# Who makes the low parts of the weight tiles: GpSimd or VectorE, in a streaming encoder block on one Trainium2 core

## The chip, the cores and the metric

The kernel runs on one core of one Trainium2 chip. The metric is device time in microseconds (us) from one launch; the times are medians of several executions. In the texts PE is TensorE, DVE is VectorE, ACT is ScalarE, POOL is GpSimd, and SP is SyncE, which here only issues transfers.

## The reference, cut to what matters

One layer of an encoder block for 512 tokens of width 1024, in float32. Three gated branches are merged, and then comes what this study is about: the output projection, a SwiGLU feed-forward part and a final norm.

```python
merged = gates[:, :, 0] * ya + gates[:, :, 1] * yb + gates[:, :, 2] * yc
x = x + merged @ w_out[l]                                   # 1024 x 1024
hf = _rms(x, g_ffn[l])
x = x + (jax.nn.silu(hf @ w_gate[l]) * (hf @ w_up[l])) @ w_down[l]   # 1024 x 2816, 2816 x 1024
return _rms(x, g_final)
```

## The kernel before, in words

**Splitting.** Each float32 matrix product is made from parts in fp32r. An operand is rounded (`hi`), and the rest `lo = x - hi` is kept as well; a product is then three matmuls, hi by hi, hi by lo and lo by hi (`product`, lines 1994 to 1996; `step`, lines 2416 to 2418, in the down projection). So each weight tile of 128 x 1024 passes four hands: SP loads it (`raw`), ACT rounds it (`w_hi`, `round_weights`, line 726; `round_unit`, line 1118), POOL or DVE subtracts (`w_lo`), and PE uses both. There are `NS = 2` slots for a tile and its parts. A load of tile t waits until the low part of tile t-2 is made (`next_weights`), and the rounding of tile t waits until PE has used tile t-2.

**Order of the tiles.** Tiles are numbered in one stream. `T_WO` to `T_WO + 7` are the eight tiles of the output projection, one for each of eight column groups `c`. `T_FF` to `T_FF + 15` are the tiles of the four "plain" pairs of the feed-forward part, four tiles a pair (gate 0, gate 1, up 0, up 1). After `T_ST` come `ST_TILES = 49` tiles for seven more pairs ("turns"), computed by a scheme with seven half-size products, and then eleven units `k` of the down projection, which share slots with the ring of the turns. A PE tile of the output projection or of a plain pair is 24 matmuls of 512 columns; a unit is 12.

**Who makes a low part.** A tile below `T_DVE = T_FF + 4` is made by POOL (`low_weights`, line 622, 128 x 1024 at once; before that `low_half`, line 627), and counted on `w_ready`. From `T_DVE` on it is DVE's: `low_plain` for the plain pairs, `low_weights(n)` for the turns, both through the helper `tt` (line 1217), counted on `w_ready_dve`. Of the units, 6 and 8 are DVE's and the other nine POOL's (line 716, in two halves with a semaphore each; unit 0 at once, line 713). `tile_low` and `low_done` turn a tile number into the count to wait for.

**DVE's program around it.** All engines run their instructions in the order written. DVE's, in order: (1) for c = 0 to 7: add the output projection's result to the residual (line 1653), make `hu_lo` (line 1657, waits for ACT's `hu_hi`), add up squares (`sqsum`, line 1217); (2) sixteen transposes of the residual (line 1664), some drains; (3) wait for `std` from ACT (line 735), RECIPROCAL to `rstd` (line 1670); (4) `scaled_gate(0, 0)` and `scaled_gate(0, 1)`, `scaled_up(0, 0)`, `low_plain(T_FF + 4)`, `scaled_up(0, 1)`, `low_plain(T_FF + 5)`, and the rest of the pairs; (5) in each turn some fifteen small combinations with `low_weights` among them; (6) `hidden_sums(10)` (four instructions of 128 x 256), `low_hidden(10)`, the low parts of units 6 and 8, then the low parts of the last stage (`low_three`).

**ACT's program around it**: for k = 0 to 7 round tile `T_WO + k + 2`, round `hu_hi`, square; round `T_FF + 2` and `T_FF + 3`; `std`; round `T_FF + 4`; SiLU; and so on. Before the units: round units 0 and 1, SiLU, units 2 and 3, `split_hidden(10)` (line 1023, waits for DVE's `hidden_sums(10)`), then the other units.

**POOL's program.** Beside the low parts POOL issues accumulating transfers between DRAM tensors (`weight_sums`, line 639), paced by waiting for each tile's low part, with three steps for each of 25 jobs. SP issues the plain copies that go ahead of them (`next_copy`, line 468), the loads of tiles (line 433 in the plain pairs) and, in the second plain pair, the eight stores of the transposed residual (`store_x1`, line 491: four behind the load of `T_FF + 4`, four behind the load of `T_FF + 5`).

**PE's program around it**: tiles `T_WO` and `T_WO + 1` interleaved, `T_WO + 2` to `T_WO + 7`, `T_FF`, a small product for the sum of squares, `T_FF + 1` to `T_FF + 15`, the turns, the units. Before each tile it waits for the tile's low part (`tile_ready`).

Of the kernel before, what the change touches and what calls it, by code (L numbers as in the profile page):

```python
# [21 lines left out]
WB = 512  # L22
# [7 lines left out]
TILE = 1024  # L30
# [16 lines left out]
T_WO = T_J2 + 14  # L47
# [4 lines left out]
T_ST = T_FF + 4 * PLAIN  # L52
T_DVE = T_FF + 4
PAIRS = KF // 2
# [5 lines left out]
R_DN = T_ST + ST_TILES  # L60
L_DN = T_DVE
GROUPS = ((0, 2), (2, 5), (5, 8), (8, 11))
# [3 lines left out]
NS = 2  # L66
# [27 lines left out]
def build(nc, xt_d, xtok_d, mem_d, mtok_d, small_d, sgu_d, row_d, w_d, ff_d, dn_d, sum_d, mix_d, half_d, x1_d, out_d):  # L94
# [7 lines left out]
    with ExitStack() as ctx:  # L102
# [63 lines left out]
        UNIT_SLOT = (0, 1, 2, 3, 4, 5, 6, 0, 1, 2, 6)  # L166
        UNIT_DVE = (6, 8)
        UNIT_POOL = tuple(k for k in range(PAIRS) if k not in UNIT_DVE)
        s1 = at("s1", o_raw, [P, 2, WB])
# [106 lines left out]
        def sems(names):  # L276
# [45 lines left out]
        unit_loaded = [sem(f"unit_loaded{i}") for i in range(7)]  # L322
        unit_half, w_ready_dve, p5_done, s1_ready, s5_ready = sems(
            "unit_half w_ready_dve p5_done s1_ready s5_ready")
        load3 = [sem(f"load3_{i}") for i in range(3)]
# [74 lines left out]
        def tile_low(eng, t):  # L400

            if t < T_DVE:
                eng.wait_ge(w_ready, t + 1)
            else:
                eng.wait_ge(w_ready_dve, t - T_DVE + 1)

        def matrices_done(eng):
# [7 lines left out]
        def _(sp):  # L415
# [72 lines left out]
            def store_x1(h):  # L488
                sp.wait_ge(x1_turned, h + 1)
                for i in range(4):  # L490
                    sp.dma_start(x1_d[KD * h:KD * (h + 1), :, i, :].rearrange("j a f -> a j f"),
                                 x1_sq[h][32 * i:32 * i + 32, :, :, :].rearrange("a j k b -> a j (k b)")
                                 ).then_inc(x1_moved, 16)

            def unit_split(eng, k):

                if k in UNIT_DVE:
                    eng.wait_ge(w_ready_dve, T_ST - T_DVE + ST_TILES + UNIT_DVE.index(k) + 1)
                else:
                    eng.wait_ge(w_ready, L_DN + UNIT_POOL.index(k) + 1)  # L500

# [113 lines left out]
        def _(pool):  # L615
# [90 lines left out]
            for n in range(0, ST_TILES, 3):  # L706
                low_done(pool, n)
                weight_sums(T_ST - NS + n // 3)
            for k in UNIT_POOL:
                pool.wait_ge(w_rounded, R_DN + k - 1)  # L710
                r, hi, lo = unit_raw[UNIT_SLOT[k]], fv(unit_hi[SPLIT_SLOT[k]]), unit_lo[SPLIT_SLOT[k]]
                if k == 0:
                    nc.gpsimd.tensor_tensor(lo, r, hi, ALU.subtract).then_inc(w_ready, 1)
                    continue
                for c, done in ((slice(WB, TILE), unit_half), (slice(0, WB), w_ready)):
                    nc.gpsimd.tensor_tensor(lo[:, c], r[:, c], hi[:, c], ALU.subtract).then_inc(done, 1)


        @block.scalar
        def _(act):  # L720
# [399 lines left out]
            def round_three(u):  # L1120

                act.wait_ge(load3[u % 3], loaded3(u))
                if u == 0:
                    act.wait_ge(w_ready, L_DN + 6)
                if u >= 2:
                    act.wait_ge(used3, u - 1)
                nc.scalar.activation(hi3[u % 2][:, 0:pieces(u), :], raw3[u % 3][:, 0:pieces(u), :], ACT.Copy  # L1127
                                     ).then_inc(rounded3, 1)
# [82 lines left out]
        def _(dve):  # L1211
# [423 lines left out]
            for g in (0, 2, 4, 6):  # L1635
# [6 lines left out]
                if g < 4:  # L1642
                    scale_gate0(g + 4)
                    scale_gate0(g + 5)

            s = norms["f"]
            dve.wait_ge(j2_lo, KD)
# [3 lines left out]
            for c in range(KD):  # L1651
                dve.wait_ge(w_used, T_WO + c + 1)
                V.scalar_tensor_tensor(xT[:, c, :], bank[c][:, :], 0.5, xT[:, c, :], ALU.mult, ALU.add
                                       ).then_inc(x1_ready, 1)
                dve.wait_ge(x1_ready, c + 5)
                dve.wait_ge(s["hi"], c + 1)
                V.scalar_tensor_tensor(hu_lo[:, c, :], xT[:, c, :], small[:, C_GFFN + c:C_GFFN + c + 1], fv(hu_hi[:, c, :]),
                                       ALU.mult, ALU.subtract).then_inc(s["lo"], 1)
                dve.wait_ge(s["sq"], c + 1)
                dve.wait_ge(s["sum"], c + 1)  # L1660
                tt(sqsum[:, :], sqsum[:, :], sq[:, c % 2, :], ALU.add).then_inc(s["sum"], 1)
# [5 lines left out]
            before(dve, ff_g, ff_u, ff_lo)  # L1667
            dve.drain().then_inc(half_stored, 16)
            dve.wait_ge(s["std"], 1)
            V.reciprocal(rstd[:, :], std[:, :]).then_inc(rstd_ready, 1)  # L1670
# [84 lines left out]

            def low_plain(t):

                dve.wait_ge(w_rounded, t - 1)
                tt(w_lo[:, t % NS, :], raw[:, t % NS, :], fv(w_hi[:, t % NS, :]), ALU.subtract).then_inc(w_ready_dve, 1)

            def low_weights(n):

                dve.wait_ge(w_rounded, T_ST + n - 1)
                tt(ring_lo[n % 3], ring_raw[n % 3], fv(ring_hi[n % 3]), ALU.subtract).then_inc(w_ready_dve, 1)

            def combine(turn, count, out, a, b, op):
# [4 lines left out]
            for n in range(2):  # L1771
                scaled_gate(0, n)
            scaled_up(0, 0)
            low_plain(T_FF + 4)
# [47 lines left out]
            for turn in range(TURNS):  # L1822
# [24 lines left out]
                if turn + 1 < TURNS:  # L1847
                    low_weights(n + 7)
                combine(turn, 12, g12, gd, u2_st[0][:, :], ALU.subtract)
                dve.wait_ge(ff_silu, 2 * i + 1)  # L1850
                combine(turn, 12, a21, a21, g11, ALU.mult)
                if turn + 1 < TURNS:
                    low_weights(n + 8)
                combine(turn, 13, a22, a22, uc_, ALU.add)
                combine(turn, 14, a11, ud, u2_st[1][:, :], ALU.subtract)
# [4 lines left out]
                tt(a11, a11, g12, ALU.mult).then_inc(ff_act, 1)  # L1860
            hidden_sums(PAIRS - 1)
            low_hidden(PAIRS - 1)

# [10 lines left out]

            for k in UNIT_DVE:
                dve.wait_ge(w_rounded, R_DN + k - 1)
                tt(unit_lo[SPLIT_SLOT[k]], unit_raw[UNIT_SLOT[k]], fv(unit_hi[SPLIT_SLOT[k]]), ALU.subtract).then_inc(w_ready_dve, 1)
            low_three(0)
# [110 lines left out]
        def _(pe):  # L1989
# [449 lines left out]
            for k in range(PAIRS):  # L2439
                if k in UNIT_DVE:  # L2440
                    pe.wait_ge(w_ready_dve, T_ST - T_DVE + ST_TILES + UNIT_DVE.index(k) + 1)
                elif k:
                    pe.wait_ge(unit_half, UNIT_POOL.index(k))
                else:
                    pe.wait_ge(w_ready, L_DN + 1)
                pe.wait_ge(ff_lo, k + 2)
                left, right = ((unit_hi[SPLIT_SLOT[k]][:, c], unit_lo[SPLIT_SLOT[k]][:, c]) for c in (slice(0, WB), slice(WB, TILE)))
                for j in range(2):
                    ins = step(6 + j, operand(1, k, j), right, k == 0, k == PAIRS - 1)
                if k == PAIRS - 1:  # L2450
                    ins.then_inc(p5_done, 1)
                if k in UNIT_POOL[1:]:
                    pe.wait_ge(w_ready, L_DN + UNIT_POOL.index(k) + 1)
                for j in range(2):
                    ins = step(4 + j, operand(0, k, j), left, k == 0, k == PAIRS - 1)
                ins.then_inc(w_used, 1)
# [181 lines left out]
```

## Time and profile before

| | us |
|---|---|
| median of 3 executions | 758.77 (756.64 to 762.88) |
| the profiled execution, its own time | 760.34 |
| its span, from first to last instruction | 758.6 |
| PE busy | 748.9 |
| POOL busy | 273.1 |
| DVE busy | 565.7 |

The profile shows one execution. Times in its rows are us from the start of the span unless marked ns; a row of the timeline gives the start, the duration, the engine, the line, the operation, what it writes and reads, how many instructions it stands for, and in brackets the idle time of the engine before it and who ended it. Outside the span lie 760.34 - 758.6 = 1.7 us.

### The profile page before, as it was taken

To read this page: it belongs to the slowest core of one execution; us is meant where nothing else is said; L and a number is where in the kernel's file an instruction comes from. 1 tells how busy PE (TensorE), PEld (TensorE's weight loads), DVE (VectorE), ACT (ScalarE), POOL (GpSimd) and SP (SyncE) were. 2 spreads that over 40 slices of the span, in tenths; PEclk is the share of its full clock that TensorE was granted. 3 is DMA by queue.
4 is the path that set the end of the run, shared out by engine and by line. 5 is a ranking of instruction groups with operands and counts; after the bars stand their busy time and mean duration, and the time that the engine had idled before them with its cause. 6 is when DMAs were issued, how large, how long until landed. Compare 5 with 4: busy or idle time off the path is not lost.

```text
span 758.6 us, 10786 instructions
## 1 busy us (share of the span) xinstructions
PE 748.9 (99%) x4066; PEld 643.8 (85%) x4066; DVE 565.7 (75%) x870; ACT 389.7 (51%) x576; POOL 273.1 (36%) x204
## 2 busy tenths in 40 slices
PE   8999999999999999999999999999999999999997
PEld 7788887788888888888788878889999999788886
DVE  6999999785857576246666679888888888536686
ACT  6896567643636343544343443454455555434554
POOL 4456665244454535446565511111000001830000
PEclk9999999999999999999999999999999999999999
DMA  8733557068575778687787898888888665867863
GB/s 289 296 144 134 199 167 235 31 198 235 149 227 163 212 214 265 195 234 222 215 235 218 245 297 244 236 259 286 246 240 256 204 212 190 313 222 255 291 199 121
DMA packets 58339, 166.77 MB, mean 220 GB/s; under 512 B 6960, under 2 KB 9136, under 8 KB 51504
## 3 DMA queue, kind: packets, MB, share of 16 engines
q1 hardware_dynamic: 53744, 139.61, 52.5%
q0 software_dynamic: 4400, 26.22, 18.1%
q8 instruction: 32, 0.52, 0.3%
q10 hardware_dynamic: 144, 0.26, 0.1%
q14 instruction: 19, 0.16, 0.1%
HBM read 158.99 MB, written 59.51 MB: 288 GB/s over the span
## 4 chain that ended last, share of the span: by engine, by line
PE 42%; POOL 21%; issue 19%; DVE 10%; ACT 4%; DMA 2%; SPq 0%; POOLq 0%; DVEq 0%; ACTq 0%
POOL w_lo L622 15%; PE bank L1994 10%; PE bank L1995 10%; PE bank L1996 10%; PE bank L2416 4%; PE bank L2418 4%; PE bank L2417 4%; POOL sum_dram L639 4%; DVE tab_tmp L1217 2%; ACT uc L786 1%; DVE s5p L1217 1%; DMA raw<-ff_dram 1%; ACT w_hi L726 1%; POOL mix_dram L639 1%; DMA xT<-xt_dram 1%
## 5 line engine op out<-in xcount | busy, mean ns | idle before, releaser
L726 ACT ACTIVATE w_hi<-raw 128x1024 fp32r<-128x1024 f32 x84 | 88.9, 1059 | 186.1 <-PE bank L1996 148.0
L622 POOL TENSOR_TENSOR w_lo<-raw,w_hi 128x1024 fp32r<-128x1024 f32 x50 | 121.6, 2432 | 144.2 <-ACT w_hi L726 144.2
L1994 PE MATMUL bank<-h_hi,w_hi 128*128 128x512 f32 (+1 forms) x480 | 164.7, 343 | 0.3 <-POOL w_lo L627 0.2
L1996 PE MATMUL bank<-h_hi,w_lo 128*128 128x512 f32 (+1 forms) x480 | 163.1, 340 | 0.0
L1995 PE MATMUL bank<-h_lo,w_hi 128*128 128x512 f32 (+1 forms) x480 | 163.1, 340 | 0.0
L1994 PEld LDWEIGHTS bank<-h_hi,w_hi 128*128 128x128 f32 x480 | 91.1, 190 | 11.1 <-issue 1.5
L1996 PEld LDWEIGHTS bank<-h_hi,w_lo 128*128 128x128 f32 x480 | 91.1, 190 | 10.1
L1995 PEld LDWEIGHTS bank<-h_lo,w_hi 128*128 128x128 f32 x480 | 91.1, 190 | 9.8 <-issue 0.2
L627 POOL TENSOR_TENSOR w_lo<-raw,w_hi 128x512 fp32r<-128x512 f32 x48 | 67.0, 1416 | 53.1 <-ACT w_hi L726 47.3
L1217 DVE TENSOR_TENSOR w_lo<-raw,w_hi 128x1024 fp32r<-128x1024 f32 x45 | 54.9, 1221 | 14.3 <-ACT w_hi L1118 5.4
L639 POOL DMA_DIRECT2D mix_dram<-mix_dram x22 | 17.2, 782 | 115.2 <-DVE w_lo L1217 85.1
L1040 ACT ACTIVATE w_hi<-raw 128x1024 fp32r<-128x1024 f32 x32 | 33.8, 1056 | 35.5 <-DMA raw<-sum_dram 20.6
L1217 DVE TENSOR_TENSOR lo<-raw,hi 128x1536 fp32r<-128x1536 f32 (+1 forms) x19 | 33.3, 1758 | 24.3 <-ACT hi L1127 24.1
L1994 PE MATMUL bank<-hu_hi,w_hi 128*128 128x512 f32 x128 | 50.3, 393 | 0.4 <-DVE w_lo L1217 0.4
L1996 PE MATMUL bank<-hu_hi,w_lo 128*128 128x512 f32 x128 | 49.8, 389 | 0.0
L1995 PE MATMUL bank<-hu_lo,w_hi 128*128 128x512 f32 x128 | 49.8, 389 | 0.0
L1995 PE MATMUL bank<-xT_r,w_hi 128*128 128x256 f32 x168 | 47.5, 283 | 0.0
L1127 ACT ACTIVATE hi<-raw 128x1536 fp32r<-128x1536 f32 (+1 forms) x19 | 27.3, 1442 | 32.0 <-PE bank L2418 27.2
L1217 DVE TENSOR_TENSOR th<-bank,rstd 128x512 f32<-128x512 f32 x16 | 10.9, 682 | 30.4 <-PE bank L1996 30.4
L1995 PEld LDWEIGHTS bank<-xT_r,w_hi 128*128 128x128 f32 x168 | 32.3, 192 | 0.0
L1994 PE MATMUL bank<-t_hi,w_hi 128*128 128x256 f32 x112 | 31.7, 283 | 0.0
L1996 PE MATMUL bank<-t_hi,w_lo 128*128 128x256 f32 x112 | 31.7, 283 | 0.0
(366 smaller groups left out, 1858.1 us busy)
## 6 DMA issues: line engine op xcount, KB each, us to landing
raw<-w_dram SPq DMA_DIRECT2D x68, 512.0 KB, 3.9
sum_dram<-ff_dram SPq DMA_DIRECT2D x28, 512.0 KB, 6.0
mix_dram<-down_dram SPq DMA_DIRECT2D x22, 512.0 KB, 7.5
raw<-sum_dram SPq DMA_DIRECT2D x37, 256.0 KB, 4.3
raw<-ff_dram SPq DMA_DIRECT2D x16, 512.0 KB, 4.6
sum_dram<-ff_dram POOLq DMA_DIRECT2D x14, 512.0 KB, 6.9
sum_dram<-sum_dram POOLq DMA_DIRECT2D x28, 256.0 KB, 5.3
raw<-ff_dram SPq DMA_DIRECT2D x27, 256.0 KB, 3.3
```

Of the source, the lines that this page charges most:

```text
L622: nc.gpsimd.tensor_tensor(w_lo[:, s, :], raw[:, s, :], fv(w_hi[:, s, :]), ALU.subtract).then_inc(w_ready, 1)
L627: return nc.gpsimd.tensor_tensor(w_lo[:, s, c], raw[:, s, c], fv(w_hi[:, s, c]), ALU.subtract)
L639: nc.gpsimd.dma_start(to, of, accum_op=ALU.add, max_dma_last_dim=8 * TILE).then_inc(done, 16)
L726: nc.scalar.activation(w_hi[:, slot, :], raw[:, slot, :], ACT.Copy).then_inc(w_rounded, 1)
L1040: nc.scalar.activation(ring_hi[n % 3], ring_raw[n % 3], ACT.Copy).then_inc(w_rounded, 1)
L1217: return V.tensor_tensor(out, a, b, op)
L1994: mm(out, a[0], b[0], start=first, stop=False)
L1995: mm(out, a[0], b[1], start=False, stop=False)
L1996: return mm(out, a[1], b[0], start=False, stop=last)
L2416: mm(bank[b][:, :], a[0], w[0], start=first, stop=False)
L2417: mm(bank[b][:, :], a[0], w[1], start=False, stop=False)
L2418: return mm(bank[b][:, :], a[1], w[0], start=False, stop=last)
```

## The change

`T_DVE` moves from `T_FF + 4` to `T_WO + 2`, so ten more tiles of the stream have their low parts made by DVE: `T_WO + 2` to `T_WO + 7` and `T_FF` to `T_FF + 3`. Eight are made inside the loop over `c`, each between the residual add and `hu_lo`; `T_FF + 2` behind the transposes and ahead of the wait for `std`; `T_FF + 3` behind the reciprocal and the two `scaled_gate`. All eleven units become DVE's, each in one instruction: 0 and 1 inside the last turn, 2 and 3 between `hidden_sums(10)` and `low_hidden(10)`, 4 to 10 behind that. The half-unit semaphore goes, and PE waits once for each unit.

```diff
-T_DVE = T_FF + 4
+T_DVE = T_WO + 2
-L_DN = T_DVE
+L_DN = T_ST - T_DVE + ST_TILES
-        UNIT_DVE = (6, 8)
-        UNIT_POOL = tuple(k for k in range(PAIRS) if k not in UNIT_DVE)
...
+        def unit_split(eng, k):
+
+            eng.wait_ge(w_ready_dve, L_DN + k + 1)
...
-            for k in UNIT_POOL:
-                pool.wait_ge(w_rounded, R_DN + k - 1)
-                r, hi, lo = unit_raw[UNIT_SLOT[k]], fv(unit_hi[SPLIT_SLOT[k]]), unit_lo[SPLIT_SLOT[k]]
-                if k == 0:
-                    nc.gpsimd.tensor_tensor(lo, r, hi, ALU.subtract).then_inc(w_ready, 1)
-                    continue
-                for c, done in ((slice(WB, TILE), unit_half), (slice(0, WB), w_ready)):
-                    nc.gpsimd.tensor_tensor(lo[:, c], r[:, c], hi[:, c], ALU.subtract).then_inc(done, 1)
...
                 if u == 0:
-                    act.wait_ge(w_ready, L_DN + 6)
+                    unit_split(act, 5)
...
                 V.scalar_tensor_tensor(xT[:, c, :], bank[c][:, :], 0.5, xT[:, c, :], ALU.mult, ALU.add
                                        ).then_inc(x1_ready, 1)
+                low_plain(T_WO + c + 2)
                 dve.wait_ge(x1_ready, c + 5)
...
             dve.drain().then_inc(half_stored, 16)
+            low_plain(T_FF + 2)
             dve.wait_ge(s["std"], 1)
             V.reciprocal(rstd[:, :], std[:, :]).then_inc(rstd_ready, 1)
...
+            def low_unit(k):
+
+                dve.wait_ge(w_rounded, R_DN + k - 1)
+                tt(unit_lo[SPLIT_SLOT[k]], unit_raw[UNIT_SLOT[k]], fv(unit_hi[SPLIT_SLOT[k]]), ALU.subtract
+                   ).then_inc(w_ready_dve, 1)
...
             for n in range(2):
                 scaled_gate(0, n)
+            low_plain(T_FF + 3)
             scaled_up(0, 0)
             low_plain(T_FF + 4)
...
                 combine(turn, 11, g21, g21, gc, ALU.add)
                 if turn + 1 < TURNS:
                     low_weights(n + 7)
+                else:
+                    low_unit(0)
                 combine(turn, 12, g12, gd, u2_st[0][:, :], ALU.subtract)
...
                 if turn + 1 < TURNS:
                     low_weights(n + 8)
+                else:
+                    low_unit(1)
...
             hidden_sums(PAIRS - 1)
+            low_unit(2)
+            low_unit(3)
             low_hidden(PAIRS - 1)
...
-            for k in UNIT_DVE:
-                dve.wait_ge(w_rounded, R_DN + k - 1)
-                tt(unit_lo[SPLIT_SLOT[k]], unit_raw[UNIT_SLOT[k]], fv(unit_hi[SPLIT_SLOT[k]]), ALU.subtract).then_inc(w_ready_dve, 1)
+            for k in range(4, PAIRS):
+                low_unit(k)
...
             for k in range(PAIRS):
-                if k in UNIT_DVE:
-                    pe.wait_ge(w_ready_dve, T_ST - T_DVE + ST_TILES + UNIT_DVE.index(k) + 1)
-                elif k:
-                    pe.wait_ge(unit_half, UNIT_POOL.index(k))
-                else:
-                    pe.wait_ge(w_ready, L_DN + 1)
+                pe.wait_ge(w_ready_dve, L_DN + k + 1)
...
-                if k in UNIT_POOL[1:]:
-                    pe.wait_ge(w_ready, L_DN + UNIT_POOL.index(k) + 1)
```

## Rows read from the trace of the kernel before

**Rows 1.** The page, part 1: busy us, share of the span, instructions.

```profile
PE 748.9 (99%) x4066; PEld 643.8 (85%) x4066; DVE 565.7 (75%) x870; ACT 389.7 (51%) x576; POOL 273.1 (36%) x204
```

**Rows 2.** Waits of PE: us in total, times, longest.

```profile
PE bank L2416 <- POOL w_lo L716: 1.0, 2, 0.5
PE bank L1994 <- POOL w_lo L622: 0.6, 1, 0.6
PE bank L1994 <- DVE w_lo L1217: 0.4, 1, 0.4
```

**Rows 3.** Timeline of PE: starts that fix the pace, and waits.

```profile
377.01 0.50 PE L1994 MATMUL bank<-mg_hi,w_hi 128*128 128x512 f32 x1 [0.63 <-POOL w_lo L622]
...
433.86 0.39 PE L1994 MATMUL bank<-hu_hi,w_hi 128*128 128x512 f32 x1
434.08 0.39 PE L1995 MATMUL bank<-hu_lo,w_hi 128*128 128x512 f32 x1
...
450.73 0.47 PE L1994 MATMUL bank<-hu_hi,w_hi 128*128 128x512 f32 x1 [0.37 <-DVE w_lo L1217]
...
657.95 0.50 PE L2416 MATMUL bank<-w_hi,ops 128*128 128x512 f32 x1 [0.54 <-POOL w_lo L716]
...
661.42 0.50 PE L2416 MATMUL bank<-w_hi,ops 128*128 128x512 f32 x1 [0.43 <-POOL w_lo L716]
```

**Rows 4.** Groups by line: the two engines' price of a low part.

```profile
L622 POOL TENSOR_TENSOR w_lo<-raw,w_hi 128x1024 fp32r<-128x1024 f32 x50 | 121.6, 2432 | 144.2 <-ACT w_hi L726 144.2
L1217 DVE TENSOR_TENSOR w_lo<-raw,w_hi 128x1024 fp32r<-128x1024 f32 x45 | 54.9, 1221 | 14.3 <-ACT w_hi L1118 5.4
```

**Rows 5.** DVE's groups by form, 380 to 422 us (output projection).

```profile
L1657 DVE SCALAR_TENSOR_TENSOR hu_lo<-xT,small,hu_hi 128x512 fp32r<-128x512 f32 x8 | 18.1, 2266 | 9.0 <-ACT hu_hi L739 9.0
...
L1217 DVE TENSOR_TENSOR sqsum<-sqsum,sq 128x512 f32<-128x512 f32 x8 | 5.4, 680 | 0.0
```

**Rows 6.** Timeline of DVE: the first plain pair, then the last turn's end.

```profile
421.50 5.33 DVE L1664 STREAM_TRANSPOSE x_sq<-xT 128x256 f32<-128x256 f32 x16
431.77 3.35 DVE L1670 RECIPROCAL rstd<-std 128x512 f32<-128x512 f32 x1 [4.93 <-ACT std L735]
435.15 1.29 DVE L1217 TENSOR_TENSOR silu<-bank,rstd 128x512 f32<-128x512 f32 x2
436.36 0.68 DVE L1217 TENSOR_TENSOR parts<-bank,rstd 128x512 f32<-128x512 f32 x1
...
449.37 1.21 DVE L1217 TENSOR_TENSOR w_lo<-raw,w_hi 128x1024 fp32r<-128x1024 f32 x1
...
652.61 1.40 DVE L1701 SCALAR_TENSOR_TENSOR parts<-odd,parts 128x256 f32<-128x256 f32 x1
```

**Rows 7.** Timeline of ACT at the same places.

```profile
428.68 1.06 ACT L726 ACTIVATE w_hi<-raw 128x1024 fp32r<-128x1024 f32 x1 [5.29 <-PE bank L1996]
...
431.05 0.69 ACT L735 ACTIVATE std<-bank,eps 128x512 f32<-128x512 f32 x1
...
654.10 1.06 ACT L1023 ACTIVATE ops<-parts 128x1024 fp32r<-128x1024 f32 x1 [3.21 <-DVE parts L1701]
```

**Rows 8.** Timeline of POOL at the same places.

```profile
429.82 2.39 POOL L622 TENSOR_TENSOR w_lo<-raw,w_hi 128x1024 fp32r<-128x1024 f32 x1 [3.22 <-ACT w_hi L726]
...
656.49 6.12 POOL L716 TENSOR_TENSOR w_lo<-raw_d,w_hi 128x512 fp32r<-128x512 f32 x4 [2.77 <-ACT w_hi L1118]
```

**Rows 9.** SP's issue of the load of `T_FF + 5`; then DMA landings, 420 to 456 us.

```profile
432.24 0.39 SPq L433 DMA_DIRECT2D raw<-ff_dram  x1
...
DMA to landing us min/median/max: 3.5/6.6/9.9
```

**Rows 10.** Timeline of PE: its last matmul.

```profile
753.11 0.28 PE L1996 MATMUL bank<-hi,second_r 128*128 128x256 f32 x1
```

**Rows 11.** Windows: PE, PEld, DVE, ACT, POOL busy (count), granted clock, DMA share, GB/s.

```profile
440.00:460.00 20.00, 19.63 (x87) 15.92 (x86) 15.34 (x23) 10.37 (x16) 2.55 (x4) 1.00 0.95 284
...
755.50:756.00 0.50, 0.00 (x0) 0.00 (x0) 0.00 (x0) 0.23 (x1) 0.00 (x0) 0.83 0.00 0
756.00:756.50 0.50, 0.00 (x0) 0.00 (x0) 0.00 (x0) 0.00 (x0) 0.00 (x0) 0.50 0.26 90
```

More of the change, by code:

```diff
@@ L322, in build @@
         unit_loaded = [sem(f"unit_loaded{i}") for i in range(7)]
-        unit_half, w_ready_dve, p5_done, s1_ready, s5_ready = sems(
-            "unit_half w_ready_dve p5_done s1_ready s5_ready")
+        w_ready_dve, p5_done, s1_ready, s5_ready = sems("w_ready_dve p5_done s1_ready s5_ready")
         load3 = [sem(f"load3_{i}") for i in range(3)]
@@ L493, in store_x1 @@
                                  ).then_inc(x1_moved, 16)
-            def unit_split(eng, k):
-                if k in UNIT_DVE:
-                    eng.wait_ge(w_ready_dve, T_ST - T_DVE + ST_TILES + UNIT_DVE.index(k) + 1)
-                else:
-                    eng.wait_ge(w_ready, L_DN + UNIT_POOL.index(k) + 1)
             def load_unit(k):
@@ L1644, in _, with low_plain @@
                     scale_gate0(g + 5)
+            def low_plain(t):
+                dve.wait_ge(w_rounded, t - 1)
+                tt(w_lo[:, t % NS, :], raw[:, t % NS, :], fv(w_hi[:, t % NS, :]), ALU.subtract).then_inc(w_ready_dve, 1)
             s = norms["f"]
@@ L1754, in low_forms_b @@
                 dve.drain().then_inc(normed, 2)
-            def low_plain(t):
-                dve.wait_ge(w_rounded, t - 1)
-                tt(w_lo[:, t % NS, :], raw[:, t % NS, :], fv(w_hi[:, t % NS, :]), ALU.subtract).then_inc(w_ready_dve, 1)
             def low_weights(n):
@@ L2439, in _ @@
             for k in range(PAIRS):
-                if k in UNIT_DVE:
-                    pe.wait_ge(w_ready_dve, T_ST - T_DVE + ST_TILES + UNIT_DVE.index(k) + 1)
-                elif k:
-                    pe.wait_ge(unit_half, UNIT_POOL.index(k))
-                else:
-                    pe.wait_ge(w_ready, L_DN + 1)
+                pe.wait_ge(w_ready_dve, L_DN + k + 1)
                 pe.wait_ge(ff_lo, k + 2)
```

## The prediction

> **What bounds the kernel now.** I read the page's busy shares first, then who PE waits for, then PE's timeline tile by tile, and only then the other engines around PE's waits. PE is busy for 748.9 of 758.6 us [rows 1], so only what makes PE wait, or ends a wait, can move the time. Its pace is fixed: in a stretch without waits matmuls of 512 columns start 0.227 us apart (434.08 against 433.86 is 0.22, and 24 of them fill 5.44 us) [rows 3]. In the whole region that the change touches the list of waits has only four for a low part: 1.0 us in two pieces in the down projection, 0.6 in the output projection, 0.4 in the plain pairs [rows 2]. POOL needs 2.43 us for a low part and DVE 1.22 [rows 4], but POOL's slowness costs nothing wherever the part is ready before PE wants it, which is a tile (5.44 us) after the tile ahead was started.
>
> A stop costs a little more than its wait: the start behind it is late against the pace, and the matmul after it by another 0.1. From the starts, the stop at 377.01 loses 0.9 us, that at 450.73 0.6, those at 657.95 and 661.42 0.8 and 0.7 [rows 3]. So 3.0 us is all that better low parts could give in the whole region.
>
> **Output projection (six tiles, and the first two of the plain pairs).** The stop at 377.01 is for T_WO + 1, which stays POOL's: it stays, 0 us gained. For the eight tiles behind it DVE gets 8 x 1.22 us inside the loop. Per column group DVE now does the residual add (no longer than sqsum, to a hundredth), 2.27 us of hu_lo and 0.68 of sqsum [rows 5]. hu_lo has as many elements as sqsum and takes 1.59 us longer: the eight of them run while POOL makes a low part, and end as it ends. With POOL's instruction gone I take hu_lo at 0.69. The loop's work is then 0.69 + 1.22 + 0.69 + 0.68 = 3.3 us, with some 0.7 of waiting for ACT's rounding, in 5.44 us of a PE tile: it keeps up, and each low part is ready 1.2 us sooner than POOL's. Nobody waited for those, so 0 us; bounds -0.1 and, if hu_lo stays at 2.27, still under 5.44 and again 0. The loads behind them start 1.2 us earlier, which also gives nothing.
>
> **T_FF + 2.** POOL had it at 425.9. DVE comes to it after the transposes, which take 5.33 us from 421.50 [rows 6] and start some 1 us sooner without the slow hu_lo: done at about 425.9, low part at 427.1. PE wants it 5.44 before T_FF + 3, at 433.86 - 5.44 = 428.4 [rows 3]. Hidden, with 1.3 us to spare; the load of T_FF + 4 starts 1.2 us later.
>
> **T_FF + 3: a new stop.** This is the step that decides. ACT has rounded the tile at 428.68 + 1.06 = 429.7 [rows 7], and POOL made the low part from 429.82 to 432.21 [rows 8], ahead of PE's need at 433.86 [rows 3]. In the changed program DVE makes it behind the reciprocal and both scaled gates. The reciprocal can't move: it waits for std, which ACT starts after rounding T_FF + 3 (itself waiting for PE) and a table load, and has at 431.05 + 0.69 = 431.74 [rows 7]. Then 3.35 us of reciprocal and 1.29 of gates; the next DVE instruction starts at 436.36 [rows 6]. There now stands the low part: 436.36 + 1.22 = 437.58, and PE starts some 0.15 later (as PE started at 450.73 [rows 3] behind a DVE part ready at 449.37 + 1.21 [rows 6]), at 437.7. PE stands from 433.86 to 437.7: 3.9 us, 4.0 with the slow second start. Both instructions ahead of it have rows, so the size is sure to a few tenths; for a lower end, if DVE could begin the low part as soon as the tile is rounded it would be 0, for an upper, +0.4 if the part takes 1.6 as DVE instructions beside POOL do.
>
> Behind it: everything in the pair is DVE's and ACT's work triggered by PE, so it moves with PE. The stop at T_FF + 6 (0.6 us) should vanish: its cause was the load of T_FF + 5, issued at 432.24 when T_FF + 3's low part was made [rows 9], landing 9.9 us later, which pushed DVE's work behind the need. Now that load starts at 437.7, with the four stores of the residual behind the load of T_FF + 4 long issued; it should land by 442 to 443, and ACT can't round it before PE is through T_FF + 3, at 443.2. PE wants T_FF + 6 at 437.7 + 3 x 5.44 = 454.0, and DVE has it at about 452. Gain 0.6, bounds 0 and 0.6.
>
> **TensorE's clock.** A row of the tail bears on the new stop: the last matmul ends at 753.39, and the granted clock is 1.00 until 755.5, 0.83 on average over the next half us and 0.50 after that [rows 10, 11]. That puts the fall from 2.4 to 1.2 GHz at 755.8, 2.4 us after PE stopped. A stop of 3.7 us is longer. No row shows how fast the clock returns; each us at 1.2 GHz does half the work and costs 0.5 us. If it returns as late as it fell, 1.2 us is lost; bounds 0 (no fall) and half a tile, 2.7. I take 1.2. The Trainium skill ("TensorE: Matmul & The Clock Gate", section "What's actually happening") says that the gate looks at TensorE's activity on a beat of its own, not tied to the kernel's start; by it the same stop would cost the clock in some executions and not in others, and a median would show one or the other. The tail shows the fall and can't show that.
>
> **Down projection.** The two stops are for units 4 and 5. The chain: while POOL makes units 2 and 3, the four instructions of hidden_sums take some 1.4 us instead of 0.4 (the last at 652.61, 1.40) [rows 6]; ACT's split_hidden waits for them until 654.10 [rows 7], units 4 and 5 are rounded behind that, and POOL makes both in one run of 6.12 us from 656.49 [rows 8]. With DVE: units 0 and 1 inside the last turn (rounded at 641.9 and 644.8, ready by 643.8 and 646.1; PE starts unit 0 at 646.3 and a unit lasts 2.72), hidden_sums done by 649.5, unit 2 at 650.7, unit 3 at 652.1 (ACT rounds it by 650.9), unit 4 at about 655, unit 5 at 657, needed at 657.2 and 660.0. Both stops go: -1.5 us, bounds -1.5 and 0. DVE's extra work is 9 x 1.22 = 11 us, where it was idle for 5 to 6 us at a time; units 6 to 10 need 1.22 in each 2.72. The combinations behind units 0 and 1 slip by up to 1.1 us, and PE needs none of them within that.
>
> **Sum.** -0 (output projection) + 4.0 (T_FF + 3) - 0.6 (T_FF + 6) - 1.5 (units) = +1.9 us, and +1.2 for the clock: +3.1. Against the profiled execution's 760.34 that is 763.4; that execution lies 1.6 over the median of 758.77. The forecast goes by the median: 761.9.
>
> **The rivals.**
> (a) The same stop, but the clock holds: +1.9, 760.7. For it: the fall came 2.4 us after the stop only once, in the tail, where PE had been less dense. Against: 3.7 is well over 2.4.
> (b) The other side: no stop at T_FF + 3, and the 0.6 + 1.5 us come back: 756.7. This needs the low part by 433.7, that is, std 3.9 us sooner. It decides at 1.9 us sooner: from there on the change is not slower. Against: std hangs on ACT's rounding of T_FF + 3, which hangs on PE, and on nothing that POOL held up. For it: only that I may misread what a wait covers.
> (c) Loads come late behind the stop. SP runs its list in order: the load of T_FF + 5 and four stores now come in one burst from 437.7, and the load of T_FF + 6 right behind at about 441. The longest landing is 9.9 us with DMA at 0.95 of its share [rows 9, 11]: landing at 451, rounded and subtracted by 453.5, just in time; three us more is a further stop of 3: 764.9. Against: DMA stands nearly idle in the stop.
> (d) The units' stops stay, because ACT and not POOL is what is late there: 763.4.
>
> **How the numbers follow.** Forecast with the clock's fall 0.40, (a) 0.32, (b) 0.10, (c) 0.14, (d) 0.04. All lie within 6 us of each other. The runs before spread from 756.64 to 762.88, so a median of a few may be off by 1 to 2 us; the range is 757.0 to 766.0, from just above (b) to (c) with 1 us of spread. About 1% (7.6 us) is what a measurement of this kernel tells from no change; faster by that would need 2.5 times all the stops there are (0.02), slower by that would need (c) and the clock's upper bound together (0.04).
>
> **What would show it.** Right: PE waits for DVE w_lo about 3.7 us once, at 434; POOL's line 716 is gone from PE's waits; hu_lo at 0.7 us; the reciprocal still at 432; a clock under 1.00 somewhere in 436 to 442. Wrong: no wait of PE near 434, a wait for a load behind it, or stops for units still there. If the time falls under 758 the stop was not there or something I call hidden was not.

## The result, and the profile after

The changed kernel takes 764.0 us (median of 6, 762.47 to 766.92) against 758.29 for the kernel before (median of 6 beside it). The ratio is 1.0068, with a 95% interval of 1.0046 to 1.0091: slower by 5.2 us by the ratio (the two medians lie 5.7 us apart). A second comparison, twelve executions of the change on another occasion, gave 1.0044 (1.0027 to 1.0060), 3.3 us. The forecast was 761.9, +3.1 to +3.6 us from the medians, in a range of 757.0 to 766.0. The profiled execution took 763.95 us, with a span of 762.2.

The page's first part shows the work moved: POOL from 273.1 us to 224.4, DVE hardly changed (it gained 19 instructions, and lost time in which POOL held it up), and PE 1.8 us longer with the same 4066 matmuls. Compare [rows 1].

```profile
PE 750.7 (98%) x4066; PEld 646.0 (85%) x4066; DVE 568.5 (75%) x889; ACT 390.2 (51%) x576; POOL 224.4 (29%) x177
```

The waits of PE in the changed kernel (us in total, times, longest), against [rows 2]: one of 3.7 us for DVE is new, and those for POOL's line 716 are gone, as is the 0.4 at T_FF + 6. The 0.6 for T_WO + 1, which the change doesn't touch, is still there in this execution.

```profile
PE bank L1993 <- DVE w_lo L1202: 3.7, 1, 3.7
...
PE bank L1993 <- POOL w_lo L616: 0.6, 1, 0.6
```

DVE's timeline in the changed kernel shows why, and PE's what it cost (lines 1202, 1662, 1993 to 1995 here are 1217, 1670, 1994 to 1996 before). Against [rows 3, 6]: T_FF + 2's part is made from 425.19 to 426.42; DVE then stands for 4.41 us until std comes, and T_FF + 3's part ends at 436.64, behind the reciprocal and the gates.

```profile
425.19 1.23 DVE L1202 TENSOR_TENSOR w_lo<-raw,w_hi 128x1024 fp32r<-128x1024 f32 x1 [0.40 <-issue]
430.83 3.35 DVE L1662 RECIPROCAL rstd<-std 128x512 f32<-128x512 f32 x1 [4.41 <-ACT std L720]
434.21 1.29 DVE L1202 TENSOR_TENSOR silu<-bank,rstd 128x512 f32<-128x512 f32 x2
435.42 1.22 DVE L1202 TENSOR_TENSOR w_lo<-raw,w_hi 128x1024 fp32r<-128x1024 f32 x1
```

```profile
436.78 0.77 PE L1993 MATMUL bank<-hu_hi,w_hi 128*128 128x512 f32 x1 [3.71 <-DVE w_lo L1202]
437.35 0.63 PE L1994 MATMUL bank<-hu_lo,w_hi 128*128 128x512 f32 x1
437.77 0.63 PE L1995 MATMUL bank<-hu_hi,w_lo 128*128 128x512 f32 x1
```

The matmuls behind the stop start 0.42 us apart and not 0.227. The windows (PE, PEld, DVE, ACT, POOL busy, granted clock, DMA share, GB/s) say that this is the clock: it falls between 435 and 436, some 2.1 us after PE's last matmul ended at 433.1, and is at 0.50 (1.2 GHz) until just before 442.

```profile
435.00:436.00 1.00, 0.00 (x0) 0.00 (x0) 1.00 (x2) 0.99 (x2) 0.00 (x0) 0.58 0.88 309
436.00:437.00 1.00, 0.22 (x1) 0.25 (x2) 1.00 (x2) 0.69 (x2) 0.07 (x1) 0.50 0.10 36
...
441.00:442.00 1.00, 1.00 (x3) 0.76 (x3) 0.00 (x0) 0.00 (x0) 0.00 (x0) 0.51 1.21 248
442.00:443.00 1.00, 1.00 (x6) 0.80 (x5) 0.00 (x0) 0.00 (x0) 0.00 (x0) 1.00 1.04 213
```

The groups of DVE in the output projection, against [rows 5], show what came free: hu_lo takes 746 ns and not 2266, so DVE, with eight low parts more, still waits 11.8 us for PE in these eight tiles.

```profile
L1202 DVE TENSOR_TENSOR w_lo<-raw,w_hi 128x1024 fp32r<-128x1024 f32 x8 | 9.8, 1226 | 3.7 <-ACT w_hi L711 3.7
L1648 DVE SCALAR_TENSOR_TENSOR hu_lo<-xT,small,hu_hi 128x512 fp32r<-128x512 f32 x8 | 6.0, 746 | 0.0
L1643 DVE SCALAR_TENSOR_TENSOR xT<-bank,xT 128x512 f32<-128x512 f32 x8 | 5.5, 692 | 11.8 <-PE bank L1995 11.8
```

In the kernel before, hu_lo starts while POOL makes a low part and ends 0.55 us behind the end of POOL's instruction, in each of the eight column groups; the prediction had it "end as it ends". The last of them:

```profile
418.03 2.40 POOL L622 TENSOR_TENSOR w_lo<-raw,w_hi 128x1024 fp32r<-128x1024 f32 x1 [2.23 <-ACT w_hi L726]
```

```profile
418.68 2.30 DVE L1657 SCALAR_TENSOR_TENSOR hu_lo<-xT,small,hu_hi 128x512 fp32r<-128x512 f32 x1 [1.16 <-ACT hu_hi L739]
```

The Trainium skill ("SBUF — State Buffer", section "SBUF: two separate sides") says that DVE, with two SBUF inputs, and POOL take turns on one pair of ports, each for a whole instruction. These rows, and the 2266 and 746 ns, agree with it.

And at the end of the last turn, against [rows 6, 7]: the four instructions of hidden_sums take 0.42 us each (before, three of the four took 1.40 to 1.51), so ACT's split_hidden starts 1.55 us after the last of them, behind only its own rounding.

```profile
654.17 0.42 DVE L1693 SCALAR_TENSOR_TENSOR parts<-odd,parts 128x256 f32<-128x256 f32 x1
```

```profile
655.17 1.06 ACT L1103 ACTIVATE hi_c<-raw_d 128x1024 fp32r<-128x1024 f32 x1 [2.40 <-DMA raw_d<-mix_dram]
656.14 1.04 ACT L1008 ACTIVATE ops<-parts 128x1024 fp32r<-128x1024 f32 x1
```

**Where the time lies.** I cut each profiled execution at four starts in PE's timeline: the first matmul of T_WO, the first of T_FF, the second of the turns (0.12 us behind the first), the first of the units. Each entry is the difference of two such starts in us.

| kernel | until T_WO | output projection | plain pairs | turns | units and what follows, to the last matmul |
|---|---|---|---|---|---|
| before | 372.0 | 44.6 | 88.7 | 141.0 | 106.8 |
| the change | 371.2 | 44.5 | 94.5 | 141.3 | 105.3 |
| the change again | 370.7 | 43.6 | 93.7 | 141.6 | 105.2 |
| early T_FF + 3 | 373.1 | 43.6 | 89.8 | 141.0 | 105.2 |
| stop filled | 371.2 | 43.6 | 92.0 | 143.6 | 105.2 |
| stop filled, again | 372.4 | 43.6 | 92.0 | 143.1 | 105.2 |
| units alone | 370.3 | 43.6 | 88.1 | 141.0 | 105.3 |
| stream alone | 372.4 | 43.6 | 93.4 | 141.0 | 105.6 |
| ahead of the gates | 371.3 | 43.6 | 92.5 | 141.0 | 105.2 |
| stores later | 370.9 | 44.1 | 88.1 | 143.6 | 105.2 |

The floor of each stage, where PE never waits, is 43.6, 88.1, 141.0 and 105.2. Before lies over it by 1.0 (T_WO + 1), 0.6 (T_FF + 6) and 1.6 (units 4 and 5): about the 3.0 us of the prediction, found again. The change lies over it by 0.9, 6.4, 0.3 and 0.1.

Other rows of the table say that these three stops are not in every execution of that code. Up to T_WO + 1 it is the same in all ten kernels, and seven of them take 43.6 us for the output projection. "Units alone" has the plain pairs of the kernel before, and takes 88.1: no stop at T_FF + 6. "Stream alone" has its units, with POOL, and takes 105.6: 0.4 over the floor and not 1.6. In "units alone" the load of T_FF + 5 lands 9.0 us after its issue (9.9 in the kernel before), and in "stream alone" POOL's run for units 4 and 5 starts 9.1 us behind the first matmul of the units, which is at 650.35 (10.2 us in the kernel before, 656.49 against 646.33). First two rows of "units alone", then one of "stream alone":

```profile
429.53 0.39 SPq L434 DMA_DIRECT2D raw<-ff_dram  x1
```

```profile
438.56 1.06 ACT L711 ACTIVATE w_hi<-raw 128x1024 fp32r<-128x1024 f32 x1 [3.63 <-DMA raw<-ff_dram]
```

```profile
659.48 6.09 POOL L716 TENSOR_TENSOR w_lo<-raw_d,w_hi 128x512 fp32r<-128x512 f32 x4 [1.40 <-ACT w_hi L1118]
```

The code ahead of T_WO is the same in all ten, and its time spreads over 2.8 us; that is one reason why medians of a few executions can't tell 1 us.

### The profile page after: what moved, and what is told of

Its sections match the earlier page's. It is cut to its first block, busy times and chain, and to the rows that moved or that the text cites. A ratio compares the mean times of both kernels' runs of the same rounds, so it can differ in the third digit from the quotient of the medians.

```text
span 762.2 us, 10779 instructions
## 1 busy us (share of the span) xinstructions
PE 750.7 (98%) x4066; PEld 646.0 (85%) x4066; DVE 568.5 (75%) x889; ACT 390.2 (51%) x576; POOL 224.4 (29%) x177
## 4 chain that ended last, share of the span: by engine, by line
PE 55%; POOL 16%; issue 16%; ACT 5%; DVE 5%; DMA 2%; SPq 0%; POOLq 0%; ACTq 0%; DVEq 0%
PE bank L1993 14%; PE bank L1994 14%; PE bank L1995 14%; POOL w_lo L616 12%; PE bank L2415 4%; PE bank L2416 4%; PE bank L2417 4%; POOL sum_dram L633 4%; ACT uc L771 2%; ACT w_hi L711 1%; POOL w_lo L621 1%; DMA raw<-w_dram 1%; DVE h_lo L1207 1%; DMA xT<-xt_dram 1%; DVE s5p L1202 1%
## 5 line engine op out<-in xcount | busy, mean ns | idle before, releaser
L616 POOL TENSOR_TENSOR w_lo<-raw,w_hi 128x1024 fp32r<-128x1024 f32 x40 | 96.3, 2409 | 122.2 <-ACT w_hi L711 122.2
L1202 DVE TENSOR_TENSOR w_lo<-raw,w_hi 128x1024 fp32r<-128x1024 f32 x58 | 70.8, 1221 | 13.7 <-ACT w_hi L711 5.4
L633 POOL DMA_DIRECT2D mix_dram<-mix_dram x22 | 17.2, 780 | 141.3 <-DVE w_lo L1202 122.1
L1993 PEld LDWEIGHTS bank<-hu_hi,w_hi 128*128 128x128 f32 x128 | 24.7, 193 | 9.5 <-issue 4.3
```

The lines of the kernel that those rows point to most:

```text
L616: nc.gpsimd.tensor_tensor(w_lo[:, s, :], raw[:, s, :], fv(w_hi[:, s, :]), ALU.subtract).then_inc(w_ready, 1)
L633: nc.gpsimd.dma_start(to, of, accum_op=ALU.add, max_dma_last_dim=8 * TILE).then_inc(done, 16)
L1202: return V.tensor_tensor(out, a, b, op)
L1993: mm(out, a[0], b[0], start=first, stop=False)
```

## The experiments

**1. The low part of T_FF + 3 made early**

```diff
             low_plain(T_FF + 2)
+            low_plain(T_FF + 3)
             dve.wait_ge(s["std"], 1)
...
-            low_plain(T_FF + 3)
             scaled_up(0, 0)
```

> The changed kernel with one call moved: the low part of T_FF + 3 directly behind that of T_FF + 2, ahead of DVE's wait for std. Theory (a stop of 3.9 us for this low part, and 2.4 us in the slow clock behind it, make the slowdown, and the rest of the change is a small gain): PE has no wait near 433, the clock stays at 1.00, the time is 764.0 - 6.3 = 757.7 or, from the other side, 758.3 - 0.6 - 1.5 = 756.2, ratio to before about 0.997 to 0.999. Rival (DVE is simply too full, or transfers paced by it come later, and the stop is only where it shows): most of the slowdown stays, 761 or more, and the wait turns up at another tile.

Measured: 759.4 us (12 executions), ratio 0.9999 (0.9988 to 1.0011). The slowdown is gone with one moved line: the stop and what follows from it are all of it, within the 0.1% of that interval. But the small gain that should have been left did not come. The trace has no wait near 433, and two others, at T_FF + 5 and T_FF + 6:

```profile
PE bank L1993 <- DVE w_lo L1202: 1.2, 2, 0.9
```

ACT's timeline gives the cause of the longer one: T_FF + 5's load, issued at 431.06 among the eight stores of the residual, lands at 443.3.

```profile
443.33 1.06 ACT L711 ACTIVATE w_hi<-raw 128x1024 fp32r<-128x1024 f32 x1 [5.65 <-DMA raw<-ff_dram]
```

```profile
428.38 2.18 SPq L492 DMA_DIRECT2D x_dram<-x_sq  x4
431.06 0.81 SPq L434 DMA_DIRECT2D raw<-ff_dram  x1
431.91 7.23 SPq L492 DMA_DIRECT2D x_dram<-x_sq  x4
```

**2. The stop filled with matmuls**

```diff
                     pe.wait_ge(free, 2 * i + 1)
+                    if (i, g, n) == (0, 1, 1):
+                        for _ in range(16):
+                            mm(bank[7][:, :], hu_hi[:, 0, 0:P], hu_hi[:, 1, :], start=True, stop=True)
                     tile_ready(4 * i + T_FF + 2 * g + n)
```

> The changed kernel with 16 matmuls of 512 columns (3.6 us) into a free bank, their result unused, ahead of PE's wait for the low part of T_FF + 3. The low part stays late. Theory (the clock falls because PE stands still, and that alone costs 2.4 us on top of the stop): the clock stays at 1.00, T_FF + 3 starts at the same place, and the time is 764.0 - 2.4 = 761.6, ratio to before 1.0045. Rival (the matmuls at 0.43 us apart behind the stop are slow for another reason, such as DMA or SBUF traffic in the burst behind the stop): they stay slow and the time stays at 764.

Measured: 764.8 us, ratio 1.0068 (1.0046 to 1.0091). In the trace the theory holds to a tenth: T_FF + 3 starts 3.8 us late as before, but its matmuls are 0.23 us apart and the clock stays up, though the same loads and stores run beside it.

```profile
432.03 3.79 PE L2342 MATMUL bank<-hu_hi 128*128 128x512 f32 x16
435.81 0.50 PE L1993 MATMUL bank<-hu_hi,w_hi 128*128 128x512 f32 x1
436.15 0.39 PE L1994 MATMUL bank<-hu_lo,w_hi 128*128 128x512 f32 x1
```

```profile
436.00:442.00 6.00, 6.00 (x27) 4.95 (x27) 2.60 (x4) 0.35 (x1) 1.65 (x2) 1.00 0.88 200
```

The plain pairs take 92.0 and not 94.5 us. So standing still, and not the traffic, is what slows the clock. The time of the whole kernel, though, did not follow (the forecast was 761.6, ratio 1.0045): the turns took 143.6 us and not 141.3. That was one trace, and 2.4 us is near what six executions can tell, so experiments 6 to 9 ask it again.

**3. Each part alone**

Units alone: `T_DVE = T_FF + 4` and the three calls of `low_plain` for the new tiles taken out of the changed kernel.

> Only the down projection's part of the change (all eleven units by DVE, T_DVE as before). Theory: the two stops of PE for units 4 and 5 go, 1.5 us, 756.8, ratio 0.998; no stop at T_FF + 3. Rival (ACT's late rounding and not POOL holds units 4 and 5): the stops stay and the time is 758.3.

Measured: 758.9 us (12 executions), ratio 0.9995 (0.9979 to 1.0011). The trace shows no wait of PE at the units (105.3 us, on the floor), as every trace with DVE there does. Whether the two stops came from POOL's own run or from the hidden_sums that it slowed is not separated. The gain of 1.5 us is not to be seen in the time; the interval holds it and holds nothing as well.

Stream alone: the kernel before with `T_DVE = T_WO + 2` and those calls put in.

> Only the other part of the change (T_DVE = T_WO + 2, with T_FF + 3 where the change puts it; units as before). Theory: stop 4.0, clock 2.4, the stop at T_FF + 6 gone (0.6): +5.8, 764.1 to 765.5, the units' two stops still there, ratio about 1.008 to 1.009. Rival (part of the slowdown comes with the units, whose low parts sit among the last turn's combinations): 1.006 or less.

Measured: 764.1 us, ratio 1.0066 (1.0049 to 1.0083), the change's own ratio, where 1.008 to 1.009 was forecast. The slowdown is this part's. The two stops at the units, forecast to be still there, are not: PE's longest wait there is 0.1 us, though POOL makes these parts as before. Here the same wait of 3.7 us cost less clock: it fell later (0.76 in 436 to 437) and was back before 440, so the plain pairs took 93.4 us.

```profile
436.00:437.00 1.00, 0.00 (x0) 0.00 (x0) 1.00 (x2) 0.99 (x2) 0.00 (x0) 0.76 0.28 96
...
439.00:440.00 1.00, 1.00 (x4) 0.81 (x3) 0.40 (x1) 0.00 (x0) 0.31 (x1) 0.54 0.51 184
440.00:441.00 1.00, 1.00 (x5) 0.80 (x5) 0.00 (x0) 0.00 (x0) 0.48 (x1) 1.00 1.01 367
```

**4. A shorter stop**

```diff
+            low_plain(T_FF + 3)
             for n in range(2):
                 scaled_gate(0, n)
-            low_plain(T_FF + 3)
             scaled_up(0, 0)
```

> The changed kernel with the low part of T_FF + 3 between the reciprocal and the two scaled gates, 1.2 us earlier than in the change. The stop becomes 2.6 us. Theory: a stop of 2.6 us is about as long as the tail needed for the clock to fall (2.4), so the clock falls late or not at all; the plain pairs take 88.1 + 2.7 = 90.8 us if it holds and up to 93 if it falls. Rival (the slow matmuls behind the stop come from the burst of transfers, not from standing still): they are as slow and as many as in the change, 11 at 0.43 us.

Measured (one execution): 761.0 us; PE waits 2.5 us, and the plain pairs take 92.5: 88.1, the stop's 2.7, and 1.7 for the clock. It falls even so, here only after PE had gone on at 434.86, and is back at 439, with eight matmuls or so slow. The forecast left both cases open, 90.8 us with the clock held and up to 93 with it fallen; it is the second.

```profile
434.00:435.00 1.00, 0.14 (x1) 0.17 (x2) 1.00 (x2) 0.81 (x1) 0.00 (x0) 1.00 1.07 376
435.00:436.00 1.00, 1.00 (x4) 0.83 (x5) 1.00 (x3) 0.65 (x2) 0.85 (x1) 0.79 0.47 153
...
438.00:439.00 1.00, 1.00 (x4) 0.80 (x3) 0.38 (x1) 0.00 (x0) 0.33 (x1) 0.51 1.11 384
```

**5. Early, and the stores out of the way**

Experiment 1, and in SP's program:

```diff
-                if i == 1 and j < 2:
+                if i == 2 and j < 2:
                     store_x1(j)
```

> The changed kernel with the low part of T_FF + 3 made early (behind that of T_FF + 2), and the eight stores of the transposed residual issued one pair later (behind the loads of T_FF + 8 and T_FF + 9, not T_FF + 4 and T_FF + 5). Theory (with the stop gone, PE waits 0.9 + 0.4 us at T_FF + 5 and T_FF + 6 because these tiles' loads are queued among the stores): both waits go, the plain pairs take 88.1 us from the first tile to the turns, 1.7 us less than with the early low part alone, ratio to before 0.997 to 0.998. Rival (the waits there come from the spread of DMA landings, whatever is stored): same time as before, waits at other tiles.

Measured: 758.8 us (12 executions), ratio 0.9989 (0.9973 to 1.0006). The theory holds where it was aimed, with no wait in the plain pairs, 88.1 us; of the ratios forecast, 0.997 to 0.998, the interval holds the upper end, and it holds no change as well. But this execution then lost 2.5 us in the turns, where nothing was changed:

```profile
579.92 1.06 ACT L1025 ACTIVATE w_hi<-raw_c 128x1024 fp32r<-128x1024 f32 x1 [3.94 <-DMA raw_c<-sum_dram]
```

```profile
581.01 1.22 DVE L1202 TENSOR_TENSOR w_lo<-raw_c,w_hi 128x1024 fp32r<-128x1024 f32 x1 [3.41 <-ACT w_hi L1025]
582.16 0.41 DVE L1202 TENSOR_TENSOR u_st<-u_st,bank 128x256 f32<-128x256 f32 x1
582.61 0.42 DVE L1202 TENSOR_TENSOR odd<-u_st,bank 128x256 f32<-128x256 f32 x1
```

```profile
583.17 0.35 PE L1993 MATMUL bank<-t_hi,w_hi 128*128 128x256 f32 x1 [2.21 <-DVE odd L1202]
```

A tile of the ring landed late, ACT waited for it, DVE waited for ACT with a low part, and behind that low part in DVE's program stood the combination that frees a bank for PE. PE's wait names `DVE odd`; two steps back it is a transfer. This version is the fastest by its ratio, but it is not shown to be faster than the kernel before.

**6. Four stops, and 7. four filled stops**

To see the clock's cost against the spread, the stop was made fourfold. In kernel 6 the low part of the last tile of each further plain pair is computed four times more before it is counted; in kernel 7 all four stops are filled with 15 matmuls as in experiment 2.

```diff
             def low_plain(t):

                 dve.wait_ge(w_rounded, t - 1)
+                for _ in range(4 if t in (T_FF + 7, T_FF + 11, T_FF + 15) else 0):
+                    link(tt(w_lo[:, t % NS, :], raw[:, t % NS, :], fv(w_hi[:, t % NS, :]), ALU.subtract))
                 tt(w_lo[:, t % NS, :], raw[:, t % NS, :], fv(w_hi[:, t % NS, :]), ALU.subtract).then_inc(w_ready_dve, 1)
```

> The changed kernel with three more stops like its own: the last tile of each of the other plain pairs (T_FF + 7, + 11, + 15) has its low part computed four times over by DVE before it is counted, some 4.9 us more, so PE should wait some 3.5 to 4.5 us at each. Theory (a stop of this length also costs about 2.4 us of slow clock): granted clock at 0.50 behind each of four stops; the three new ones cost 3 x (4 + 2.4) = 19 us, 783. Rival (the time without the clock's loss, because later waits for transfers swallow it): 3 x 4 = 12, 776.

> The same four stops, each filled with 15 matmuls of 512 columns (3.4 us) into a free bank, result unused. Theory: the clock stays at 1.00, and the time is 4 x 2.4 = 9.6 us under that of the kernel with four bare stops. Rival (what the clock takes is given back by later waits): less than 4 us under it. This is the fourfold of a difference that one stop leaves inside the spread.

Measured (4 executions each): 775.1 us bare, ratio 1.0196 (1.0170 to 1.0222), and 770.9 filled, 1.0147 (1.0117 to 1.0177). The difference of 4.2 us is under the 9.6 of the theory and just over the rival's 4. In the two traces only 2.1 us of the difference lie in the plain pairs (104.7 against 102.5); as much lies ahead of them, where the two kernels are the same. Two sizes were off. The new waits were shorter than meant:

```profile
PE bank L1995 <- DVE w_lo L1202: 11.2, 4, 3.7
```

that is 3.7, 2.9, 2.5 and 2.2 us. Fifteen matmuls take 3.4 us, so filling lengthened the three new stops. And the clock fell behind two of them only, the first and the third (windows of the bare kernel around the second and the third):

```profile
464.00:466.00 2.00, 0.59 (x3) 0.53 (x4) 1.97 (x4) 0.04 (x1) 0.44 (x1) 1.00 0.00 0
466.00:468.00 2.00, 2.00 (x11) 1.65 (x10) 2.00 (x4) 1.92 (x4) 0.35 (x1) 1.00 0.68 188
...
489.00:491.00 2.00, 0.99 (x4) 0.86 (x5) 2.00 (x2) 0.00 (x0) 0.77 (x1) 1.00 0.01 4
491.00:493.00 2.00, 2.00 (x7) 1.56 (x6) 1.93 (x4) 0.00 (x0) 0.00 (x0) 0.58 0.93 255
```

The second stop, 2.9 us, kept the clock; the third, 2.5 us, lost it. The Trainium skill says that the gate looks on a beat of its own ("TensorE: Matmul & The Clock Gate", section "What's actually happening"); the trace agrees: the longer of two stops went free. In the plain pairs the bare kernel takes 104.7 us: 88.1, stops of 11.9 by their starts, and 4.7 for the clock.

**8. Four stops, filled to size**

The three new stops filled with 9 matmuls and not 15.

> The four stops filled again, but with 9 matmuls (2.0 us) in the three new ones, whose waits were only 2.2 to 2.9 us, so that filling them no longer lengthens them; 15 in the first. Theory (the clock's loss reaches the end of the kernel): the plain pairs take 104.7 - 4.8 = 99.9 us, 2.6 less than with 15 everywhere, and the time is 770.9 - 2.6 = 768.3, some 6 under the four bare stops (775.1), ratio to before 1.011 to 1.012. Rival (later waits for transfers give it back): within 3 us of the bare stops, 772 or more.

Measured (6 executions, on another chip than the bare stops): 771.5 us, ratio 1.0154 (1.0120 to 1.0188), 3.6 under the bare stops; the forecast of 768.3 fails, and the rival's 772 is missed by half a us. The trace shows one reason: filled and at full clock, the three new stops are 3.5, 2.6 and 3.5 us by their starts, against 3.0, 2.7 and 2.3 in the bare kernel (the waits here are only what the fill leaves).

```profile
PE bank L1995 <- DVE w_lo L1202: 3.2, 4, 1.3
```

My reading: the late low part comes by DVE's own program, which doesn't wait for PE alone, so a PE that lost time to the clock finds the next part less late. In the traces 4.7 us of slow clock cost only 2.5 in the plain pairs (104.7 against 102.2).

**9. The change and its filled stop, side by side**

> The changed kernel once more, on one chip with the same kernel with its stop filled, since the two first came out alike (1.0068 both) though the plain pairs took 94.5 us in the one trace and 92.0 in the other. Here 1.006 to 1.007, plain pairs 93.4 to 94.5 us (stop 3.9, clock 1.3 to 2.4).

> The changed kernel with its stop filled by 16 matmuls, once more. Theory (what the clock costs reaches the end of the kernel): 1.3 to 2.4 us faster than the bare stop on the same chip, ratio about 1.004. Rival (swallowed by later waits): the same ratio as the bare stop, 1.006 to 1.007.

Measured, 12 executions each on one chip: bare 763.7 us, 1.0044 (1.0027 to 1.0060); filled 763.5 us, 1.0042 (1.0025 to 1.0058). The bare kernel was forecast at 1.006 to 1.007 and is under that; the 1.004 forecast for the filled one is met, but by the bare one too. The theory falls: the two means lie 0.2 us apart, with a 95% interval from -0.6 to 1.1, worked out from the two sets of twelve, so the clock's loss, 1.7 us in this pair of traces, does not reach the end. The waits of PE behind the plain pairs, first of the bare, then of the filled kernel:

```profile
PE bank L1993 <- DVE w_lo L1202: 0.4, 1, 0.4
```

```profile
PE bank L1993 <- DVE odd L1202: 1.5, 1, 1.5
```

Twice now the filled kernel led by 2.5 and 1.7 us at the start of the turns and gave back 2.3 and 1.4 in them (table above). In the second of the two, the wait of 1.5 us is the one of experiment 5, for a transfer two steps back. In the first, the largest piece is another, 0.8 us for a low part, and the rest comes in small steps:

```profile
536.68 0.38 PE L1993 MATMUL bank<-h_hi,w_hi 128*128 128x256 f32 x1 [0.80 <-DVE w_lo L1202]
```

That PE waits there because it comes sooner is not shown: "units alone" and "early T_FF + 3" reach the turns sooner still, at 501.9 and 506.4 us, and wait for nothing in them. What is shown is that filling the stop leaves the time as it is.

## Why the prediction was right, point by point

**The stop at T_FF + 3** was forecast at 3.9 us, 4.0 with the slow second start, from the ends of the reciprocal and the gates. Measured: 3.86 by the starts, a wait of 3.71. Experiments 1 and 4 show that it follows the place of one call in DVE's program. This term carried the forecast.

**The clock** was the mis-sized term: 1.2 us by the forecast, with 2.7 as its upper bound. Within the bound, it cost 2.5 in the change's trace (6.4 over the floor less 3.86), 1.7 in its second, 1.4 with the stream alone and 1.7 behind the shorter stop. "If it returns as late as it fell" was the failing step: in the change's first trace the clock fell 2.1 us after PE had stopped and was back only 5.2 us after PE had gone on. It stays low for 3.4 us in some runs and 6.8 in that one, and PE stands only in part of that. Rival (a), the clock holds, did not occur at this stop in any trace; a single stop of 2.9 us elsewhere shows that it can.

**The gains**, 0.6 at T_FF + 6 and 1.5 at the units, are in the change's trace with just these sizes (table). I took them as gains of the kernel. Units alone (0.9995) and the early part (0.9999) show that hardly any of it arrives in the time; an effect under 1 us can't be told. The table has a reason that I left out: I read both stops from one execution, which at 760.34 us is 2 us over the median of 758.29. Of the same code, "units alone" (at T_FF + 6) shows 0 and "stream alone" (at the units) 0.4 us. One trace of each can't tell how often the stops come. Beside that, the turns, in which DMA is busy for 0.83 to 0.89 of the time in the first four of the seven and for less behind them (kernel before), take from 0 to 2.6 us over their floor in these ten traces.

**So the sum** of +3.1 came out as +3.6 in the two profiled executions, made of 5.8 in the plain pairs, -1.5 at the units, +0.3 in the turns, -0.1 in the output projection and -0.8 ahead of T_WO, where nothing was changed; and as +5.2 and +3.3 in the two comparisons. Two of my errors, too little clock and gains that don't arrive, and one in the other direction, a clock loss of which experiment 9 finds nothing in the time, work against each other, so that the sum came near is in part luck. One figure of the prediction is wrong as it stands: its rivals lie from 756.7 to 764.9, within 8.2 us of each other and not 6.

**The output projection and T_FF + 2** went as forecast: hu_lo at 0.75 us (0.69 forecast), the eight parts made in time, T_FF + 2's at 426.4 in a trace that runs 0.9 us ahead (427.1 forecast). **Rival (c)**, late loads behind the stop, did not occur: T_FF + 5 was rounded as soon as PE let it. It occurred in experiment 1, where the stop was taken away. **Rival (b)** is refuted by the wait, and **(d)** by the units' floor in the change itself and in experiment 3.

What stays open: whether units alone, experiment 1 and experiment 5 are faster than the kernel before at all, and what decides when a load in the turns comes late. Their medians lie between 0.2 us over and 0.8 under it, and every interval holds no change.

## What to carry to other kernels

When an engine takes over a small step of another, ask at each place what stands ahead of the step in its program: here nine of ten moved tiles and all units were free, and the tenth, put behind a reciprocal that waits for two engines, cost more than all the rest could give. In these kernels one stop of TensorE of 2.5 or 3.7 us cost 1.4 to 2.5 us more in slow clock within its stage, and two, of 2.2 and 2.9 us, cost nothing more; filling the stop with unused matmuls kept the clock in every trace, and gained nothing that the time shows. And a stop of 1 us seen in one trace is not yet a stop of the kernel: take the time of each stage from several traces, those of other versions with the same code there among them.

## What the runs showed that I had not expected

The granted clock fell anywhere from 2.1 to 4.9 us after PE stopped, and in three traces only after PE had gone on; of two stops of 2.9 and 2.5 us in one execution the shorter one lost it. Twelve executions of the same change had a mean granted clock of 0.994 to 0.998, with the stop filled 0.997 to 1.000. And 1.7 to 2.5 us saved in the middle of the kernel were missing from its time; in the two traces PE waited for 1.4 to 2.3 us more in the turns, 100 to 150 us behind the stop.
